# Two mixer stages of a five-engine kernel: head weights folded into ScalarE's copies, squares on ScalarE, lagged low halves

## What is computed

```python
proj = rms_norm(h, g) @ w_in              # 256 x 2916
cq, ckv, kr = low-rank query (192), low-rank key/value (128), shared rotary key (32), each rms-normed with its weight
fox, moba, diff = q, k, v of 4 heads each # q and k rms-normed per head with a weight, moba and diff partly rotated
mem = q of 4 heads                        # keys and values come from a memory of 256 rows
out = concat(attention(fox), attention(mla), attention(moba), attention(diff1) - lam * attention(diff2), attention(mem)) @ w_o
```

## Time and profile before

| | before |
|---|---|
| median of 3 runs | 1662.05 us |
| the profiled execution | 1665.06 us |
| its span | 1663.8 us |
| TensorE matmul busy | 1504.5 us (90%), 10862 instructions |
| VectorE busy | 1062.7 us (64%), 1533 instructions |
| ScalarE busy | 741.0 us (45%), 1151 instructions |
| GpSimd busy | 190.5 us (11%), 164 instructions |
| mean granted TensorE clock | 0.947 |

### The profile page before, as it was taken

One profiled execution on the slowest core, in us unless ns is written; L12 is line 12 of the kernel. 1 busy time (PEld: TensorE's weight loads), 2 busy tenths in 40 slices (PEclk: granted clock), 3 DMA queues, 4 the chain that ended last, 5 costly groups with the idle time before them and its releaser, 6 DMA issues. The chain is left out here.

```text
span 1663.8 us, 26062 instructions
## 1 busy us (share of the span) xinstructions
PE 1504.5 (90%) x10862; PEld 1419.4 (85%) x10862; DVE 1062.7 (64%) x1533; ACT 741.0 (45%) x1151; POOL 190.5 (11%) x164
## 2 busy tenths in 40 slices
PE   6877987999998787999999969899999978899999
PEld 5865877999997577999997759799999767899999
DVE  4653547765467846665467775577766776577763
ACT  5322324444346434444345545444445554454443
POOL 0002332110000002110001200010100110010100
PEclk9888988999999989999999988899999997899999
DMA  7431303555544323655544321255565421145563
GB/s 236 129 100 51 102 1 115 165 185 190 184 153 154 124 77 102 196 183 178 190 161 156 125 76 48 80 195 181 175 202 178 153 76 48 59 145 182 173 199 105
DMA packets 186389, 230.07 MB, mean 138 GB/s; under 512 B 5920, under 2 KB 161056, under 8 KB 186016
## 3 DMA queue, kind: packets, MB, share of 16 engines
q1 hardware_dynamic: 185264, 221.99, 41.3%
q0 software_dynamic: 1008, 6.41, 1.1%
HBM read 227.34 MB, written 1.05 MB: 137 GB/s over the span
## 5 line engine op out<-in xcount | busy, mean ns | idle before, releaser
L766 DVE TENSOR_TENSOR weights_low<-weights_raw,weights_high 128x1024 fp32r<-128x1024 f32 (+3 forms) x421 | 509.7, 1231 | 363.3 <-ACT weights_high L664 362.8
L664 ACT CAST weights_high<-weights_raw 128x1024 fp32r<-128x1024 f32 (+3 forms) x421 | 424.3, 1030 | 325.3 <-PE bank L493 323.3
L491 PE MATMUL bank<-hT_high,weights_high 128*128 128x256 f32 (+1 forms) x1672 | 487.5, 292 | 39.3 <-DVE hT_low L849 21.5
L492 PE MATMUL bank<-hT_low,weights_high 128*128 128x256 f32 (+1 forms) x1672 | 482.7, 289 | 0.0
L493 PE MATMUL bank<-hT_high,weights_low 128*128 128x256 f32 (+1 forms) x1672 | 482.2, 288 | 0.0
L491 PEld LDWEIGHTS bank<-hT_high,weights_high 128*128 128x128 f32 (+1 forms) x1672 | 330.3, 198 | 47.0 <-issue 30.2
L492 PEld LDWEIGHTS bank<-hT_low,weights_high 128*128 128x128 f32 (+1 forms) x1672 | 330.1, 197 | 0.4
L493 PEld LDWEIGHTS bank<-hT_high,weights_low 128*128 128x128 f32 (+1 forms) x1672 | 329.7, 197 | 0.4
L491 PE MATMUL bank<-aT_high,weights_high 128*128 128x256 f32 x864 | 241.8, 280 | 0.2
L492 PE MATMUL bank<-aT_low,weights_high 128*128 128x256 f32 x864 | 241.6, 280 | 0.0
L493 PE MATMUL bank<-aT_high,weights_low 128*128 128x256 f32 x864 | 241.2, 279 | 0.0
(11 more groups left out here) (409 smaller groups left out, 1928.5 us busy)
## 6 DMA issues: line engine op xcount, KB each, us to landing
weights_raw<-in_w_up SPq DMA_DIRECT2D x32, 1024.0 KB, 5.3
weights_raw<-in_w_down SPq DMA_DIRECT2D x32, 1024.0 KB, 5.0
weights_raw<-in_ffn_w_gate SPq DMA_DIRECT2D x22, 1024.0 KB, 5.2
weights_raw<-in_ffn_w_up SPq DMA_DIRECT2D x22, 1024.0 KB, 5.2
weights_raw<-in_w_in SPq DMA_DIRECT2D x20, 1024.0 KB, 5.0
weights_raw<-in_w_in_ab SPq DMA_DIRECT2D x16, 1024.0 KB, 5.7
weights_raw<-in_ffn_w_down SPq DMA_DIRECT2D x16, 1024.0 KB, 5.0
weights_raw<-in_w_o SPq DMA_DIRECT2D x10, 1024.0 KB, 5.5
```

The lines of the kernel that those rows point to most:

```text
L491: k.E.matmul(out, xh, wh, start=first, stop=False)
L492: k.E.matmul(out, xh, wl, start=False, stop=False)
L664: k.A.copy(w.halves(n)[0], w.raw_part(n)).then_inc(*k.s.weight_high(n))
L766: k.V.tensor_tensor(low, w.raw_part(n), high.bitcast(F32), ALU.subtract).then_inc(*k.s.weight_low(n))
```

## The change

- The head weights of fox, mla, moba, diff and mem become columns (one number per partition), and ScalarE applies them as the scale of the copy to `QK`. The weights of cq and ckv go the same way into the copies to `cT`. Rotated elements still need theirs before the rotation: VectorE multiplies kr and the rotated elements alone (32 of 96 for mla, 16 of 64 for moba, 8 of 32 for diff); their places in the columns hold ones.
- All copies to `QK` and to `PT` in this mixer, and the two to `kva`, are ScalarE's. The squares too; cq, ckv and kr are squared in one instruction, "low".
- GpSimd's function for this mixer is gone; the pair sums of the next stage are left.
- The order of the groups is 0 fox, 1 mla, 2 diff first half, 3 diff second half, 4 moba, 5 mem. So `work(2)` is diff, `work(3)` is empty, `work(4)` is moba, and the group without output products is 2.
- VectorE's `last_columns`: `mla_turned` comes ahead of `vector_split(n2 + 1)`, and each later low half is split one call later than its high half.
- ScalarE's `last_columns`: the copies of columns 2048 to 2559 come one call earlier, in front of the copies to `QK` of mla, with diff's squares behind them.

```diff
@@ Attention
     def by_scalar(self, n, block):
-        return (n + block) % 2 == 0
+        return self.copies_by_scalar or (n + block) % 2 == 0
@@ scalar_heads_turned
-    for c in range(0, g.blocks, 4):
+    for c in range(0, g.blocks, 2 if a.copies_by_scalar else 4):
...
+            k.A.activation(dst, bank, ACT.Copy, scale=g.gains[0:g.width, 2 * c // g.blocks:2 * c // g.blocks + 1]).then_inc(*k.banks.read(key))
@@ scalar_mixer_2
+    def squared(name, x):
+        i, width = SQUARED.index(name), x.shape[-1]
+        if i >= 2:
+            A.wait_ge(*s.reduced.at((l, SQUARED[i - 2])))
+        A.activation(shaped(m.squares[i % 2][:, 0:NT * width], NT, width), x, ACT.Square).then_inc(*s.feature_squares((l, name)))
+    squared("memk", k.kvm[l][:, :, 0:256])
     projected(0)
     scalar_root(k, (st, "memk"), m.st2[:, :, 12:16])
+    squared_columns("low", 0, 352)
...
     projected(1024)
+    squared_columns("fox", C_FOX, 512)
...
+    squared("mla_q", m.qa)
+    squared("mla_kv", m.kva)
@@ scalar_mixer_2, last_columns
         scalar_split(k, n2 + 1)
-        yield
         for t in range(NT):
             evacuated(2048, t)
+        squared_columns("diff", C_DIFF, 512)
+        yield
         scalar_split(k, n2 + 4)
...
         scalar_split(k, n5 + 3)
+        squared_columns("moba", C_MOBA, 512)
         yield
         for t in range(NT):
             evacuated(2560, t)
+        squared_columns("memq", C_MEM, 256)
         scalar_split(k, n5 + 4)
@@ vector_mixer_2, normed
-        then(V.tensor_tensor(x4, x4, spread(ss, 3, x4.shape[-1]), ALU.mult))
-        V.tensor_tensor(x, x, spread(row(name), 1, NT), ALU.mult).then_inc(*s.normed((l, name)))
+        over = V.tensor_tensor(x4, x4, spread(ss, 3, x4.shape[-1]), ALU.mult)
+        if not turned:
+            over.then_inc(*s.normed((l, name)))
+            return
+        then(over)
+        gain = spread(per_head(row(name), n, x4.shape[-1])[:, :, 0:turned], 1, NT)
+        V.tensor_tensor(x4[:, :, :, 0:turned], x4[:, :, :, 0:turned], gain, ALU.mult).then_inc(*s.normed((l, name)))
@@ vector_mixer_2, last_columns
         mla_normed()
         yield
+        mla_turned()
         vector_split(k, n2 + 1)
-        mla_turned()
         yield
         vector_split(k, n2 + 4)
-        for i in range(1, 5):
-            yield
-            vector_split(k, n5 + i)
+        yield
+        yield
+        vector_split(k, n5 + 1)
+        yield
+        vector_split(k, n5 + 2)
+        yield
+        vector_split(k, n5 + 4)
@@ vector_mixer_2, work
         if n == 2:
+            squared(DIFF)
+            scaled(DIFF)
+            turned_heads("diff", C_DIFF, 16, 32, ROT_D, ROT_C + ROT_A + ROT_M)
+        elif n == 4:
             squared(MOBA)
             scaled(MOBA)
             turned_heads("moba", C_MOBA, 8, 64, ROT_M, ROT_C + ROT_A)
-        elif n == 3:
-            squared(DIFF)
-            scaled(DIFF)
-            turned_heads("diff", C_DIFF, 16, 32, ROT_D, ROT_C + ROT_A + ROT_M)
```

More of the change, by code:

```diff
@@ L41 @@
 C_CQ, C_CKV, C_KR, C_FOX, C_FF, C_MOBA, C_DIFF, C_MEM = 0, 192, 320, 352, 1120, 1124, 1892, 2660
-OUT_2 = [2, 0, 4, 6, 8]
+HEADS_2 = ["fox", "mla", "moba", "diff", "mem", "cq"]
+OUT_2 = [2, 0, 6, 4, 8]
 FEATURES_AB = [("qkv_a", 0), ("qkv_a", 256), ("qk_b", COL_QB), ("qkv_a", 512), ("qk_b", COL_QB + 256), ("qkv_a", 768),
@@ L65 @@
     (("b_qkv", 1536), ("sinks", CH)),
-    (("cq", 192), ("ckv", 128), ("kr", 32), ("fox", 512), ("moba", 512), ("diff", 512), ("memq", 256),
-     ("memk", 256), ("mla_q", 384), ("mla_k", 256), ("sub", 256), ("fox_b", 4), ("lambda", 128)),
+    (("kr", 32), ("moba", 512), ("diff", 512), ("mla_q", 384), ("sub", 256), ("fox_b", 4), ("lambda", 128)),
 ]
@@ L2205, with heads_2 @@
 SLOT = {"cq": 0, "ckv": 1, "kr": 2, "fox": 3, "moba": 11, "diff": 19, "memq": 35}
-SQUARED = ["memk", "cq", "ckv", "kr", "fox", "mla_q", "mla_kv", "moba", "diff", "memq"]
+SQUARED = ["memk", "low", "fox", "mla_q", "mla_kv", "diff", "moba", "memq"]
+def heads_2(k, l, name):
+    c = COLS["heads2"] + l * 13 + 2 * HEADS_2.index(name)
+    return k.cols[:, c:c + (3 if name == "cq" else 2)]
 def attention_2(k, l):
@@ L2355, in scalar_mixer_2 @@
         A.copy(m.qa[:, t, :], k.banks[st, "qa", t][:, 0:384]).then_inc(*k.banks.read((st, "qa", t)))
+    for t in range(NT):
+        A.wait_ge(*s.products.at((st, "kva", t)))
+        A.copy(m.kva[:, t, :], k.banks[st, "kva", t][:, :]).then_inc(*k.banks.read((st, "kva", t)))
+    for t in range(NT):
+        A.wait_ge(*k.banks.was_read((st, "qa", t)))
+        A.wait_ge(*k.banks.was_read((st, "kva", t)))
+    squared("mla_q", m.qa)
+    squared("mla_kv", m.kva)
     def last_columns():
@@ L2378, in work @@
         if n == 2:
+            roots("diff", 19, 16)
+        elif n == 4:
             roots("moba", 11, 8)
[L2380 to L2381 removed]
         elif n == 5:
@@ L2406, in reduced, with reduced_low @@
         V.tensor_reduce(dst, src, AXX, ALU.add).then_inc(*s.reduced((l, name)))
+    def reduced_low():
+        src = shaped(m.squares[SQUARED.index("low") % 2][:, 0:NT * 352], NT, 352)
+        V.wait_ge(*s.feature_squares.at((l, "low")))
+        for c0, n, d, name in LOW_RANK:
+            last = V.tensor_reduce(m.st[:, :, SLOT[name]:SLOT[name] + 1], src[:, :, c0:c0 + d].unsqueeze(2), AXX, ALU.add)
+        last.then_inc(*s.reduced((l, "low")))
     def inverses(name, x, inv):
@@ L2474, in vector_mixer_2 @@
     projected(1536)
-    for t in range(NT):
-        V.wait_ge(*s.products.at((st, "kva", t)))
-        V.tensor_copy(m.kva[:, t, :], k.banks[st, "kva", t][:, :]).then_inc(*k.banks.read((st, "kva", t)))
     V.wait_ge(*s.products.at((st, "fc")))
```

148 lines of the change are left out of this document (68 added, 80 removed).

## The result

| | before | after |
|---|---|---|
| median | 1661.43 us (4 runs) | 1644.02 us (4 runs, 1639.38 to 1644.57) |
| ratio | | 0.9895, 95% interval 0.9862 to 0.9928 |
| span of the profiled execution | 1663.8 us | 1637.9 us |
| VectorE busy | 1062.7 us | 1024.2 us |
| ScalarE busy | 741.0 us | 778.5 us |

The change makes the kernel 17.4 us faster, 1.05%. Lines have moved: 499 is now 500, 2073 is 2077, 1872 is 1873.

What follows compares the result with a forecast made beforehand. Up to 39 us a mixer hang on TensorE's waits, mostly for VectorE. 9.3 - 0.6 = 8.7 a mixer, 17.4 for two, takes 1665.1 to 1647.7; 3 lower for the median: 1645 us, range 1624 to 1661.

Steps and rivals of the forecast that it cites:

- Mla's rotation first: Before group 1's transposes: rotation put ahead of the low half ends near 955.8, so TensorE's 2.9 us wait goes.
- Diff first, the hole closes: Diff's chain ends 3.9 us earlier, TensorE waits 3.5 us; group 0 is divided at once, last bank free at 979.8.
- It opens again: First output product: TensorE stands 7.2 us for VectorE's moba chain and group 1's division, begins at 999.4, 13.2 us earlier.
- The clock at the stall: Around the first output product: half speed lasts to 1006, so the product ends at 1008.5 against 1020.2.
- The end of the phase: From group 3's values to group 4's output product: 37.0 us against 35.1, 1.9 given back, leaving 9.3 ahead.
- Memk's squares: On ScalarE before the root that VectorE's factor needs; TensorE waits for that factor: 0.6 us added.
- the rest of VectorE's relief: Copies and weight products taken off VectorE in the phase, beyond the counted terms: slack, no gain counted.
- GpSimd's squares going: A VectorE low half beside GpSimd's squares took 2142 ns where its like took 890: 1.25 us on the path saved.
- Rival 3: ScalarE becomes the bound in steps 2 to 6, its copies late: 24 us for both mixers, 1686 us; chance 0.11.
- Rival 1: The clock stays up, none of the new waits bringing 1.2 GHz: 21 us more saved, 1624 us; chance 0.17.
- Rival 2: Gain eaten by half speed after the 966.9 wait (3 to 4 us) and through both last products (3): 1658; chance 0.22.
- Rival 4: Each square needs another table on ScalarE, loads of 1283 ns: 3.8 us a mixer, 1653 us; chance 0.04.

Runs made afterwards that it cites:

- second profile: The changed kernel run once more, unchanged, beside the others on the same chip: 1645.49 us, ratio 0.9896.
- the order alone: Kernel before with only the two difference groups put ahead of the moba group; copies, GpSimd squares, weights and lag as before: 1664.07 us, ratio 1.0011.
- squares on GpSimd and the old order: Changed kernel with the second mixer's norm squares on GpSimd again and moba's group ahead of the two difference groups again: 1643.79 us, ratio 0.9890.
- five parts undone: Changed kernel with group order, low halves' lag and place, shared copies, moba's and diff's weights on VectorE, and squares on GpSimd put back: 1662.98 us, 1.0005.
- squares on GpSimd: Changed kernel with all squares of the second mixer's norms on GpSimd again, the rest kept: 1638.14 us, ratio 0.9840.
- moba ahead: Changed kernel with moba's norm (columns' copy, squares, root and VectorE's chain) drawn forward by one step: 1635.93 us, ratio 0.9834.

## Why the prediction was right, and where not

The forecast was 1645 us, the median is 1644.0. The profile of the changed kernel confirms most of the steps; where I compare positions, after's phase begins 2.05 us sooner (scores of group 0 at 944.20 against 946.25), which I add.

- **Mla's rotation first.** No idle before group 1's transposes, as predicted. Alone it is worth less than its 2.9 us a mixer: with it undone both mixers took 0.5 us more and the kernel 2.8, for the wait behind absorbs most of it.
- **Diff first, the hole closes.** Wait at the difference's transposes 3.5 predicted, 3.59 measured. Group 2's scores follow without a hole. VectorE divides group 0 at 976.73, so 978.78, against "near 980", and group 2's exponentials end at 984.60, so 986.65, against 986.5.
- **It opens again.** Output product predicted at 999.4, measured 997.78 + 2.05 = 999.83. The stall is 4.70 us, not 7.2, because TensorE arrives later, not because VectorE is earlier: it waits 1.66 us for the last columns, and half speed starts in front of the stall, near 986, not behind it.
- **The clock at the stall.** Predicted to 1006, measured 1004 + 2.05.
- **The end of the phase** is the term that was mis-sized. From the start of the output product to the wait for line 777 I had 3.9 us given back (13.2 ahead, then 9.3); the stretch took 60.50 us (1058.28 - 997.78) against 60.96 before (1073.60 - 1012.64), so nothing was. The waits of ScalarE's copies (1.68) and exponentials (3.49) are there, against 2.6 and 3.6; the two banks' 1.3 are not (0.17), and the half speed that I charged with 5.5 us is 5 us at 0.66, or 1.7.
- **Memk's squares** were to add 0.6 to the wait for the factor: 2.17 against 1.69. The cover for cq's and fox's squares held.

The sum was 9.3 for each mixer, less 0.6 for a wait that lies ahead of the factor's product. By the second profile, from that product on, the first mixer gained 8.9 (176.1 - 167.2) and the second 12.5 (176.1 - 163.6): 9.3 and the end's 4.3 make 13.6, and the first lost 3.2 in front of the phase (last section). The stage between them gave 2.4 back (212.0 against 209.6 us), in code that did not change. Terms of opposite sign bring the sum back to its figure. That the forecast came within 1 us is luck; what it missed is 2 to 4 us each time.

**What I had wrong is the cause.** The prediction tells the gain as a story of the order: a division no longer behind a norm's chain. The stall did move as told, but the kernel with the order alone is no faster, and without it most of the gain stays. It calls "the rest of VectorE's relief" slack; copies, weights and lag together are 19 us (with the squares on GpSimd and the old order, and with up to 5.8 us of a collision in them), though in the changed kernel each alone can be undone for 3 at most. And it credits 1.25 us for GpSimd's squares going; moving them costs 7 to 9 us in all. I had their 1.0 and 0.6 us in ScalarE's path to 991.0, but never asked what the path is without them. In thousandths the chain of runs reads: 1000.5 with five parts undone, 989.0 with lag, copies and weights in, 984.0 with the new order too, and back to 989.6 with the squares on ScalarE.

The prediction also reads its row on GpSimd too softly. It sets the 1.25 us against all 8.2 us of GpSimd's work in the phase, as if the one lengthened low half spoke against full exclusion. Exclusion costs only what overlaps, 1.38 us there, and 1.25 of it were lost. The sum is the same, but it matters for the order alone, where a second such product meets the low halves.

Rival 3 had a true part: ScalarE is on the chain, though busy for 8.3 us of a step of 13.5 by the phase's mean (70.88 / 115.30), far below TensorE. It decides by its place, not by its load. Rival 1's size was in part right: the clock came back, in the last spell. Rival 2 depends on the execution: behind the wait of 3.59 us half speed held for 3 us in the first profile (1.5 us lost), but from 971.96 to 978 in the second, some 3 us lost, as it says; its second part, half speed through both last products, did not come. Rival 4 fell: the 12 table loads at the roots' line are as many as in the earlier trace rows, and none stands at a square's:

```profile
L697 ACT ACT_TABLE_LOAD x12 | 15.4, 1283 | 0.2
L2350 ACT ACTIVATE squares<-hp 128x1024 f32<-128x1024 f32 x4 | 4.2, 1054 | 0.0
```

So the Trainium skill's list, in "ScalarE: Activation LUTs", section "Table sets", of the functions that every set has, which does not name the square, is no reason to expect a load for it between copies and exponentials. The kernel does have four loads more, 52 against 48, but elsewhere: with the new order a mixer has one more turn from root to exponentials (line 1944, 11 instead of 9), and ends on exponentials, so the next stage's root needs a load (line 738, 7 instead of 5). The prediction has no term for them, and no run prices them.

What stays open: which of lag, copies and weights makes the rest of the 19 us. I undid all three with the squares on GpSimd and the old order, and each in the changed kernel; no pair, and never one and all in the same kernel.

## What to carry to other kernels

When two engines hand a chain back and forth (high half, low half, norm, root, rotation), work moved from one to the other need not be a relief: follow the chain through both queues with and without the moved instruction, and try a third engine that is idle, even at twice the duration, at a place where it does not run beside VectorE's links. Undo parts one by one and all together, in the same kernel: here parts that cost 0 to 3 us each to undo were worth 19 us as a group in another one, so "nothing alone" does not mean "nothing", and a run that puts one part alone into the old kernel can bring a collision of its own. Look at who waits for whom, which busy shares don't tell.

## What of the hardware was unexpected

**Some of VectorE's instructions all but stand still beside GpSimd's products.** What VectorE's instruction lost and how long the two overlapped: 0.86 us of 0.99 (squares on GpSimd), 1.25 of 1.38 (before), and with five parts undone 1.62 of 1.77 for a copy that is 0.23 us long. It goes both ways: in the kernel with the order alone the second of two squares took 2.55 us instead of 1.89, while low halves ran in between. Others lose nothing: before, three instructions of line 2012 (from 948.53 us), which read a bank of PSUM and `X`, and two maxima behind them took 1.88 and 1.80 us beside GpSimd's products with head weights, and as much in the changed kernel, where GpSimd is idle.

**A copy with a scale per partition costs more.** ScalarE's copies to `QK` with the weights took 668 to 690 ns, a plain one of the same kernel 576: 0.1 us each, where I had bounded it by 0.04. The group of the changed kernel, whole span:

```profile
L1928 ACT ACTIVATE QK<-bank,cols 128x512 f32<-128x512 f32 (+1 forms) x24 | 14.8, 678 | 7.0 <-PE bank L500 7.0
```

**The clock falls in code that didn't change.** Behind the mixer both kernels have the same two waits, 1.46 and some 1.9 us. Before, full speed held from there on; in the changed kernel's second profile it did not:

```profile
1083.00:1100.00 17.00, 17.00 (x135) 16.78 (x136) 13.27 (x17) 7.78 (x10) 1.50 (x3) 1.00 0.66 228
```

```profile
1072.50:1078.00 5.50, 5.50 (x34) 5.48 (x35) 4.10 (x5) 2.07 (x3) 0.16 (x2) 0.69 0.74 232
```

That is 1.7 of the stage's 2.4 us; 0.3 is the wait for the second mixer's factor (0.66 us instead of 0.37), and the rest isn't located. The stage took 211 to 212 us in nine of the profiles, and 207.4 to 210.3 in that of before and in four others. I found no rule for it, and this spell alone does not sort them: it is there with moba ahead too (0.72 over the 6 us behind the second wait), where the stage took 209.8. In the same way the wait for the factor, 2.18 us instead of 1.69, is followed by products at half speed in the second profile:

```profile
895.82 0.97 PE L651 MATMUL bank<-consts,factor 1*128 1x1 f32 x4 [2.18 <-DVE factor L821]
...
897.30 0.63 PE L493 MATMUL bank<-weights_low,hT_high 128*128 128x512 f32 x1
```

They take 0.63 us each up to 902 us; in the kernel before they take 0.39 to 0.40 there. The first scores of group 0 come 51.9 us after the factor, against 48.8: 3.2 us lost, and 1.6 in the first profile of the same kernel. The longer wait isn't shown to be the cause, since the kernel with the old order and squares on GpSimd lost 1.6 there too, behind a wait of 1.68. Between the two profiles of the changed kernel (spans 1637.9 and 1644.1 us) 3.8 us of the difference lie in the mixers, as far as the rows show in such spells.
